# Conditioning vectors of two layers: tile sums on VectorE in place of one-row products on TensorE, and an earlier first projection

## What is computed

```python
for i in range(DEPTH):                                   # DEPTH = 2
    mod = jax.nn.silu(c) @ ada_w[i] + ada_b[i]           # c: (1, 1024), ada_w[i]: (1024, 3072)
    shift, scale, gate = jnp.split(mod[:, None, :], 3, axis=-1)
    u = x * (1 + scale) + shift
    y = mixer_dilated(u, ...) if i % 2 == 0 else mixer_mla(u, ...)
    x = layernorm(DEEPNORM_ALPHA * x + gate * y, ln_g[i], ln_b[i])
...
def mixer_dilated(u, w_in, w_out, rel_bias):
    q, k, v, gate = jnp.split(u @ w_in, 4, axis=-1)      # each 1152 wide, 384 for each of 3 groups
    ...
```

## Time and profile before

| | |
|---|---|
| median of 3 executions | 4022.1 us (4016.5 to 4024.59) |
| the profiled execution: its time | 4017.8 us |
| its span, first to last instruction | 4015.8 us |
| TensorE busy | 3837.7 us, 96% |
| VectorE busy | 2232.7 us, 56% |
| GpSimd busy | 1906.1 us, 47% |
| ScalarE busy | 1454.2 us, 36% |
| mean granted clock of TensorE | 0.982 |

### The profile page before, as it was taken

How to read it: one execution, slowest core, us unless ns; L and a number is a source line. 1 busy time by engine, 2 the same in 40 slices (tenths; PEclk the granted TensorE clock), 3 DMA queues, 4 the chain that set the end, 5 groups by cost and what they waited for, 6 DMA issues and landing times.

```text
span 4015.8 us, 49833 instructions
## 1 busy us (share of the span) xinstructions
PE 3837.7 (96%) x19191; PEld 3114.5 (78%) x19191; DVE 2232.7 (56%) x3490; ACT 1454.2 (36%) x2934; POOL 1906.1 (47%) x1675
## 2 busy tenths in 40 slices
PE   8999999999999999899898999999999898999998
PEld 4677778777888887788677788888778576888887
DVE  2242336482777775653637777724644638777533
ACT  1132223132666663325534333312225534333211
POOL 1313123282333333522424788887332426788975
PEclk9999999999999999999899999999999899999999
DMA  5312211232000002210023222453210022222543
GB/s 180 116 52 78 71 49 57 78 112 66 5 8 9 9 9 69 95 40 22 24 77 97 84 80 84 141 182 113 95 43 22 28 95 93 82 79 83 178 160 125
DMA packets 245204, 310.37 MB, mean 77 GB/s; under 512 B 38548, under 2 KB 156708, under 8 KB 244968
## 3 DMA queue, kind: packets, MB, share of 16 engines
q1 hardware_dynamic: 212152, 231.87, 18.6%
q10 hardware_dynamic: 32816, 75.32, 5.5%
HBM read 253.48 MB, written 51.53 MB: 76 GB/s over the span
## 4 chain that ended last, share of the span: by engine, by line
PE 74%; DVE 16%; ACT 4%; issue 3%; POOL 1%; DMA 1%; ACTq 0%; SPq 0%; DVEq 0%; POOLq 0%
PE ps L130 70%; PE ps L133 4%; DVE ml_p L142 3%; DVE cst_sm L153 3%; ACT thi L136 2%; DVE da_sg L159 1%; DVE tlo L142 1%; DVE f_ta L150 1%; DVE f_tb L150 1%; ACT ml_o L136 1%; ACT tfi L136 0%; DVE cst_sm L150 0%; POOL mlo_z L142 0%; POOL mix_z L142 0%; ACT m_junk L136 0%
## 5 line engine op out<-in xcount | busy, mean ns | idle before, releaser
L139 POOL CAST whi<-wst 128x512 fp32r<-128x512 f32 (+2 forms) x508 | 420.1, 827 | 1343.5 <-DMA wst<-in_a_w_in 454.0
L142 POOL TENSOR_TENSOR wlo<-wst,whi 128x512 fp32r<-128x512 f32 (+2 forms) x634 | 930.6, 1475 | 40.8
L130 PE MATMUL ps<-whi,thi 128*128 128x512 f32 (+3 forms) x1816 | 710.6, 391 | 17.6 <-ACT c_rn L136 5.2
L130 PE MATMUL ps<-whi,tlo 128*128 128x512 f32 (+3 forms) x1816 | 686.4, 378 | 0.0
L130 PE MATMUL ps<-wlo,thi 128*128 128x512 f32 (+3 forms) x1816 | 685.9, 378 | 0.0
L130 PEld LDWEIGHTS ps<-whi,thi 128*128 128x128 f32 x1816 | 345.2, 190 | 99.5 <-issue 26.0
L130 PEld LDWEIGHTS ps<-wlo,thi 128*128 128x128 f32 x1816 | 345.4, 190 | 57.7 <-issue 3.8
L130 PEld LDWEIGHTS ps<-whi,tlo 128*128 128x128 f32 x1816 | 344.7, 190 | 58.1
L130 PE MATMUL ps<-thi,whi 128*128 128x512 f32 x856 | 340.8, 398 | 15.9 <-POOL wlo L142 12.3
L130 PE MATMUL ps<-thi,wlo 128*128 128x512 f32 x856 | 337.6, 394 | 0.0
L130 PE MATMUL ps<-tlo,whi 128*128 128x512 f32 x856 | 337.5, 394 | 0.0
(11 more groups left out here) (392 smaller groups left out, 8203.8 us busy)
## 6 DMA issues: line engine op xcount, KB each, us to landing
wst<-in_w_down SPq DMA_DIRECT2D x140, 256.0 KB, 3.2
wst<-in_w_up SPq DMA_DIRECT2D x126, 256.0 KB, 2.9
scr_h<-f_tb SPq DMA_DIRECT2D x44, 512.0 KB, 4.0
wst<-in_w_in SPq DMA_DIRECT2D x80, 256.0 KB, 2.7
wst<-in_a_w_in SPq DMA_DIRECT2D x72, 192.0 KB, 2.4
wst<-in_ada_w SPq DMA_DIRECT2D x48, 256.0 KB, 3.2
da_am<-in_ada_w SPq DMA_DIRECT2D x48, 256.0 KB, 2.6
f_T2lw<-scr_h SPq DMA_DIRECT2D x48, 256.0 KB, 3.6
```

The source lines that it names most:

```text
L130: return self.none if self.e is None else self.e.matmul(*a, **k)
L139: return self.none if self.e is None else self.e.tensor_copy(*a)
L142: return self.none if self.e is None else self.e.tensor_tensor(*a)
```

## The change

The sums over the eight tiles of a vector go from TensorE to VectorE: `dve_weigh` multiplies each 128 x 512 tile by `cc`'s number of each partition and adds it to an accumulator in SBUF, waiting for its own result each time. TensorE then sums over the 128 partitions, once for each vector: four products with a column of ones for shift and scale, which give columns at once (`pe_columns`), one product with a 128 x 128 matrix of ones for each half of the gate (`pe_gate_sum`), one product with one column of ones for each half vector of layer 1 (`pe_second`, now after steps 11, 23 and 35; the weighing is in four of every six steps up to 36, and the bias after steps 13, 25 and 37). The query projection of group 0 takes all six tiles in one pass over the planes, in banks 0 to 5, and starts when half 0 is made; half 1 is made between planes 3 and 4. SP loads the queries' first four weight tiles between the two halves. A slot with a tile of `ada_w` now comes free when VectorE has used it. ACT makes `thi` from `xT` with scale and bias itself, and VectorE writes the modulated planes to `tfl`. The copies of the last four row blocks of x stand behind and between the weighing of half 0 on VectorE. `cb`, `mrow` and the loads of the gate's bias into all 128 partitions go.

```diff
-        self.cb = c.new("cb", [128, 8, 128])
...
-        for h in range(2):
-            for which in range(2):
-                key = ("row", h, which)
...
-                    q.matmul(ps[0:1, b, :], self.cc[:, k:k + 1], self.wst[:, s, :], start=(k == 0),
-                             stop=(k == 7)).then_inc(*S.up("tile", ("w", w)))
...
+    def pe_columns(self, q, h):
...
+            q.wait_ge(*S.at("m_use", ("ada0", h, which, 7)))
...
+            for i in range(4):
+                ins = q.matmul(self.ps[:, b, i:i + 1], self.amb[:, which, blk(i)], self.ones[:, 0:1], start=True, stop=True)
...
+        copies(0, 1, 2, 3)
         q.wait_ge(*S.at("silu"))
...
+        self.dve_ada0(q, 0, 0)
+        copies(4, 5)
+        self.dve_ada0(q, 0, 1)
+        copies(6, 7)
...
         for h in range(2):
+            for which in range(2):
+                if h:
+                    self.dve_ada0(q, 1, which)
...
+    def dve_weigh(self, q, acc, w, k, key, first):
+
+        S, c = self.S, self.cc[:, k:k + 1]
+        if first:
+            q.tensor_scalar(acc, w, c, None, ALU.mult).then_inc(*S.up("m_use", key))
+        else:
+            q.stt(acc, w, c, acc, ALU.mult, ALU.add).then_inc(*S.up("m_use", key))
+        q.wait_ge(*S.at("m_use", key))
...
+    def pe_gate_sum(self, q, h):
...
+        q.matmul(self.ps[:, b, :], self.ones[:], self.gate[0][:, half(h)], start=True, stop=True).then_inc(*S.up("tile", key))
...
+            if h == 0:
+                for k in range(4):
+                    self.load(sp, ("aq", 0, k), [(0, self.a_columns(0, 0, k))])
...
-                if k == 1:
+                if k == 2 and n > 0:
+                    self.sp_second_store(sp, n - 1)
+                if k == 5:
                     if n > 0:
-                        self.sp_second_store(sp, n - 1)
                         sp.wait_ge(*S.at("st_m", n - 1))
...
+    def second_at(self, g, i):
+
+        j, u = i // 6, i % 6
+        return 3 * g + j // 2, 4 * (j % 2) + u - 1
...
+        q.matmul(self.ps[0:1, b, :], self.ones[:, 0:1], self.am, start=True, stop=True).then_inc(*S.up("tile", ("ar", n)))
...
+            self.pe_tiles(q, ("aq", 0), 8, items_T(3, 4), 6, "q6", made, lambda k: ("aq", 0, k), lambda it: [],
+                          lambda k, it: S.at("lo", ("x", k)), amid=lambda _, k: self.pe_columns(q, 1) if k == 4 else None)
...
         self.pe_tiles(q, ("ak", g), 8, items_T(3, 4), 4, "proj", made, lambda k: ("ak", g, k), ready)
+        if g == 0:
+            for h in range(2):
+                self.pe_gate_sum(q, h)
...
-            if g < 2 and i < 24:
-                self.pe_second(q, 24 * g + i)
+            if g < 2 and i in (11, 23, 35):
+                self.pe_second(q, self.second_at(g, i)[0])
...
-            if g < 2 and i in (8, 16, 24):
-                self.dve_second(q, 3 * g + i // 8 - 1)
+            if g < 2 and i in (13, 25, 37):
+                self.dve_second(q, self.second_at(g, i)[0] - 1)
+            if g < 2 and i < 36 and 1 <= i % 6 <= 4:
+                self.dve_second_weigh(q, *self.second_at(g, i))
```

More of the change, by code:

```diff
@@ L729, in pe_start @@
         self.pe_turn(q, "ab", [self.ab[:]], "tr4", [S.at("ld_ab")])
-        q.wait_ge(*S.at("silu"))
         q.wait_ge(*S.at("set", "ones"))
-        for h in range(2):
-            for which in range(2):
-                key = ("row", h, which)
[L735 to L742, removed]
-                    q.matmul(ps[0:1, b, :], self.cc[:, k:k + 1], self.wst[:, s, :], start=(k == 0),
-                             stop=(k == 7)).then_inc(*S.up("tile", ("w", w)))
[L745 to L754, removed]
+        self.pe_columns(q, 0)
+    def pe_columns(self, q, h):
+        S, B = self.S, self.B
+        for which in range(2):
+            col = ("col", h, which)
+            b = B.take(col, "r2")
+            q.wait_ge(*S.at("m_use", ("ada0", h, which, 7)))
+            for event in B.freed(col):
+                q.wait_ge(*event)
+            for i in range(4):
+                ins = q.matmul(self.ps[:, b, i:i + 1], self.amb[:, which, blk(i)], self.ones[:, 0:1], start=True, stop=True)
+            ins.then_inc(*S.up("turned", col))
     def act_start(self, q):
@@ L771, in act_start @@
         for h in range(2):
[L772 to L776, removed]
+            q.wait_ge(*self.B.done(("col", h, 1)))
             for k in range(4 * h, 4 * h + 4):
-                q.wait_ge(*S.at("x_mod", k))
-                q.activation(self.thi[:, k, :], self.xT[:, k, :], ACT.Copy).then_inc(*S.up("hi", ("x", k)))
-        q.dma_start(self.gate[0][:], I["ada_b"][0, 2048:3072].partition_broadcast(128)).then_inc(*S.up("ld_ada", 0, 16))
+                q.activation(self.thi[:, k, :], self.xT[:, k, :], ACT.Identity, scale=self.mc[:, 8 + k:9 + k],
+                             bias=self.mc[:, k:k + 1]).then_inc(*S.up("hi", ("x", k)))
     def dve_start(self, q):
@@ new lines, in dve_ada0, with sp_weighed @@
+    def dve_ada0(self, q, h, which):
+        S = self.S
+        if h:
+            q.wait_ge(*S.at("turned", ("col", 0, which)))
+        for k in range(8):
+            w = ("ada0", h, which, k)
+            s = self.slot(w)
+            q.wait_ge(*S.at(f"w{s}", w))
+            self.dve_weigh(q, self.amb[:, which, :], self.wst[:, s, :], k, w, k == 0)
+    def sp_weighed(self, sp, key, ap):
+        self.load(sp, key, [(0, ap)])
+        self.freeing[self.slot(key)] = [lambda: self.S.at("m_use", key)]
@@ L829, in pe_ada @@
         for k in range(8):
[L830 to L843, removed]
+            w = ("ada", h, k)
@@ L847, in sp_dilated, with dve_gate_sum @@
+            s = self.slot(w)
+            q.wait_ge(*S.at(f"w{s}", w))
+            self.dve_weigh(q, self.gate[0][:, half(h)], self.wst[:, s, :], k, w, False)
+    def dve_gate_sum(self, q, h):
+        key = ("gsum", h)
+        q.wait_ge(*self.S.at("tile", key))
+        q.tensor_copy(self.gate[0][:, half(h)], self.ps[:, self.B.of(key), :]).then_inc(*self.B.free(key, "evac_v"))
     def sp_dilated(self, sp):
@@ L912, in dve_second @@
         row = self.mst
-        q.wait_ge(*S.at("tile", ("am", 8 * n + 7)))
+        q.wait_ge(*S.at("tile", ("ar", n)))
         q.wait_ge(*S.at("ld_mb", n))
@@ L1200, in dve_dilated @@
                       ALU.add).then_inc(*B.free(("tb", n), "evac_v"))
+            for h in range(2):
+                self.dve_gate_weigh(q, h)
         else:
@@ L1211, in dve_dilated @@
             q.tensor_copy(*self.scatter_T(self.ak, g, *it, B.of(key))).then_inc(*B.free(key, "evac_v"))
+        if g == 0:
+            for h in range(2):
+                self.dve_gate_sum(q, h)
         n = (256, 320, 128)[g]
```

84 lines of the change are left out of this document (42 added, 42 removed).

## The result

The changed kernel takes **3972.4 us** (median of 4 executions, 3970.35 to 3974.72) against 4022.12 before: ratio 0.9881, 95% interval [0.9866, 0.9895]. The forecast was 3975.0, the range 3958 to 3997. The profiled execution took 3970.35 us with a span of 3968.2. The total is right, and its closeness is luck: of its two terms the loops gave 5.8 us more than forecast and the start, between the two profiled executions, 6.4 us less.

What follows compares the result with a forecast made beforehand. The prediction took TensorE, 74% of the chain of waits, to bound the kernel. Loops -44.3, crowding +1 and start -3.4 summed to -46.7 us, forecast 3975 us against the median of 4022.1; range 3958 to 3997.

Steps and rivals of the forecast that it cites:

- the loops: Loops of groups 0 and 1: one-row products leave TensorE, -50.8 us, six sums come back, +6.5; net -44.3, with crowding -43.3.
- the start: Up to the first scores: one-row and gate products leave TensorE, nearly all paid back as waits and slow clocks; -3.4 us.
- the product's true price: In the loops, removing one one-row product frees 1.13 us (group 0) or 0.99 us (group 1), more than its own 0.87.
- the weighing hidden: In the loops, four VectorE weighings per six steps, 3.2 us in a period of 15, are hidden if in time.
- The 1 us of crowding: In the loops, small delays of scores behind a weighing, priced at 1 us (0 to 12).
- the bound: The start's upper bound: weighings beside GpSimd's splits at 1.3 us each add 11 us, so the start costs +7.6.
- The slow start: In the start, TensorE restarts before plane 0 at the 1.2 GHz clock level after a pause, losing 3.1 us.
- the Trainium skill's rule: Throttled clock is the default and activity releases it, so all three restarts are slow; first transposes at clock 1.00 seemed against it.
- no slow starts: Rival in the start: the clock holds over TensorE's pauses, start -12.7, total -56 us, 3966 us; chance 0.20.
- VectorE crowds the loop: Rival in the loops: weighings wait for late tiles and delay scores, 19 us in 48 places, 3993 us; chance 0.23.
- VectorE becomes the bound: Rival in steps 1 to 4 of each six: 48 weighings at 1.3 us on the path, +25, 4047 us; chance 0.03.
- Nothing comes of it: Rival: the one-row products ran beside a wait that stays, so the time stays 4022 us; chance 0.04.

Runs made afterwards that it cites:

- thin_weigh: Changed kernel with seven of each eight layer 1 weighings in the loops cut from 512 columns to 8; 3970.7 us.
- loop_only_b: Second run of the loops' part of the change on the start of the kernel before; 3977.5 us.
- thin_gate_tail: Changed kernel with the last five gate tiles loaded and weighed with 64 of their 512 columns; 3969.9 us, one execution.
- start_only: The start's part of the change with the loops of the kernel before; 4024.49 us, ratio 1.0009 to the kernel before.
- gate_loops: Changed kernel with layer 0's gate made in the loops of groups 0 and 1 instead of the start; 3963.5 us, 3962.1 over eight executions.
- hybrid_b: The kernel of hybrid run once more; 3964.3 us.
- hybrid: From gate_loops, half 1's shift and scale made by one-row products on TensorE, half 0's by VectorE's weighing; 3966.0 us.

## Why the prediction was right

**The loops, -43.3 forecast, -49.1 measured.** The mechanism held by its steps: the product's true price read off the periods, the sums at 1.08 (0.86 to 1.05), the weighing hidden (the period of 15.04, and `thin_weigh`). Why a product frees 1.13 us when it takes 0.87 no run here tests; the change of operands that the prediction names is argued. Three sizes were off. Group 1's period without products is 15.64 us, not the 15.87 that I took from a late period of the loop, and with products it was 21.88 to 22.16, so I priced its gain too low. The 1 us of crowding did not come. And the end of group 0's loop went with the clock: before, it fell there (0.69 in the mean of 292 to 296 us), and the last period was 14.15 us; after, it fell only later, and it is 12.61. That gave 1.5 us that belong to no term. It may be chance: the changed loops have 12.6 in both traces of the changed kernel, but 14.1 in `thin_weigh` and 17.85 in `loop_only_b`; the old loops have 14.2 in both of theirs.

**The start, -3.4 forecast, +3.0 measured between the two traces.** This is the part that failed. The old start's other trace came 3.5 us later, so the size of the miss against it isn't settled; but every station of the new start was late against its own forecast, by four steps, in order:
- Plane 0 at 45.4 us, not 40.8. Copies ended at 20.96 (+0.9; the transposes' slow first stretch, below, lasted to 19.4 us instead of 18.0); scale's weighings beside GpSimd's splits cost 7.06 instead of 5.5 (+1.5), which I had kept for the bound; the bias columns, priced at 1.6, took from 39.03 to 42.77 (+2.1), because four products of one column (eight records) stand on the chain for each of the two vectors, at a clock of 0.50.
- The slow start behind it cost about 2.2 us, not 3.1 (72 products in 18.6 us for 16.4).
- Plane 4 at 77.86, not 72.0: the ring's slot is what was late, as forecast (SP issues scale's tile right behind plane 3), but the tile took 4.39 us, not 3.2, and columns and plane took 5.0 instead of 3.45.
- The keys at 112.16, not 103.8. The gate's sixth tile was weighed at 104.0 (4.5 late, all inherited), and the key tile then took 6.14 us instead of 2.7. I had taken the median landing of its kind for a tile issued behind 1.31 MB of others; `thin_gate_tail` shows that this was the cause. The first split and its start took another 0.5 us more than priced.

Behind the keys the slow clock cost half of what I gave it (it was back at 115.1 us), and the two gate sums took 1.3 us instead of 1.9, so the rest was some 2 us shorter than priced: -3.4 + 8.4 - 2.0 is the +3.0 measured.

**The clock.** All three restarts were slow, as the forecast took it and as the Trainium skill's rule (TensorE: Matmul & The Clock Gate, Part 1) has it; *no slow starts* falls. The row that seemed to speak against the rule was misread. Three stretches of transposes in the changed kernel, columns as in rows 7:

```profile
14.00:17.00 3.00, 3.00 (x16) 3.00 (x15) 1.92 (x3) 0.00 (x0) 0.00 (x0) 1.00 0.87 274
...
19.50:20.70 1.20, 1.20 (x13) 1.20 (x12) 1.17 (x3) 0.00 (x0) 0.00 (x0) 1.00 0.68 256
...
28.00:31.00 3.00, 3.00 (x16) 3.00 (x15) 2.93 (x6) 0.00 (x0) 0.00 (x0) 0.50 1.05 381
```

The first has as many transposes in 3 us as the third, whose clock is 0.50; the second has 13 in 1.2 us, twice the pace. So the first transposes ran slow, and the 1.00 beside them is no measurement: the trace's records of the clock begin only at 19.4 us (18.0 in the kernel before, where 16 transposes stand in 14 to 17 us too), and a stretch without a record shows as 1.00. The rule and this row agree, and the row that the rival *no slow starts* rested on never spoke for it.

**Other rivals.** *VectorE crowds the loop* and *VectorE becomes the bound* fall with the period of 15.04 us, which four weighings left unchanged, and with `thin_weigh`: nothing of the 22.8 us taken from VectorE reached the periods. *Nothing comes of it* falls with the periods. By the marks the gain is the loops' alone; the start, which is most of the diff, shows no gain in them.

**What stays open.** Eight executions of the loops' part alone have a median of 3977.5 us, where the marks give 4021.6 - 49.1 = 3972.5. Three lie at 3965 to 3970 and five at 3977 to 3980; in the one with a trace the two places where the clock fell, in the start and at the end of group 0, put it 8.6 us behind. And eight executions of the whole change have a median of 3973.2, 4 us below the loops alone, where `start_only` would put it 3 above. So the start's worth lies somewhere between 4 us gained and 3 lost, and whether start and loops act on each other, through where the clock falls, no run here separates.

## What to carry to other kernels

A one-row product of a float32 tile costs TensorE as much as a full one; where another engine has slack beside a loop, let it multiply and add the tiles and leave TensorE one product with ones. Move such work to where it is hidden and its result is only just needed: the same weighing that was free in the loops stood, with its loads, before three pauses of TensorE in the start, and moving the gate out of the start as well was worth another 10 us (`gate_loops`, 3962.1). When you place a load, price its landing by the bytes issued just ahead of it, not by the median of its kind.

## What the hardware showed that I had not expected

- After pauses of 1.1 to 1.8 us in a loop, alike in their length, the clock fell in one execution and not in the other, and stayed at 0.50 for some 20 us while TensorE was busy for all of it (`hybrid_b` 438 to 458 us) or all but 1.2 us (`loop_only_b` 272 to 290). `hybrid` and `hybrid_b`, one kernel, differ by 5.7 us in that place alone. Sizes under some 10 us are therefore read from marks next to the change, before the stages behind blur them: `thin_gate_tail`'s 2.9 us and half of `gate_loops`' 15 had gone by the end of the span.
- A clock of 1.00 in the first microseconds of a profile can be the lack of a record. The pace of like instructions tells: 16 transposes in 3 us at the slow level, 13 in 1.2 us at the fast one.
- A multiply-add of 128x512 in SBUF, 0.76 us alone, took 0.88 to 1.38 beside GpSimd's splits, and two of GpSimd's casts beside it 0.96 instead of 0.50.
- One execution in some eighty took four times as long as its fellows (16494 us). Its cause stays open, and it did not come back.
